# One matmul for both halves of the operand in the feed-forward input products of a float32 transformer stack

## The reference

```python
# first block
h2 = rms_norm(x, norm2_g)                                  # x * rsqrt(mean(x*x) + 1e-6) * norm2_g
x = x + jnp.square(jax.nn.relu(h2 @ w_ff1)) @ w_ff2        # 1024 -> 4096 -> 1024
# second block, in each of its two layers
x = layer_norm(ALPHA * x + swiglu(x, w_gate, w_up, w_down), g, b)
def swiglu(x, w_gate, w_up, w_down):                       # 1024 -> 2816 -> 1024
    return (jax.nn.silu(x @ w_gate) * (x @ w_up)) @ w_down
```

## Time and profile before

| | |
|---|---|
| time, median of 3 runs | 1293.88 us (1293.78 to 1297.35) |
| time of the profiled execution | 1296.51 us |
| its span, first to last instruction | 1294.7 us |
| PE busy | 1277.6 us (99%) |
| POOL busy | 947.9 us (73%) |
| ACT busy | 644.8 us (50%) |
| DVE busy | 411.5 us (32%) |
| PE's share of the chain that ended last | 96% |
| instructions on PE (matmul, and as many weight loads) | 8551 |
| HBM read | 216.07 MB |

### The profile page before, as it was taken

How to read it: one execution, slowest core, us unless ns; L and a number is a source line. 1 busy time by engine, 2 the same in 40 slices (tenths; PEclk the granted TensorE clock), 3 DMA queues, 4 the chain that set the end, 5 groups by cost and what they waited for, 6 DMA issues and landing times.

```text
span 1294.7 us, 20311 instructions
## 1 busy us (share of the span) xinstructions
PE 1277.6 (99%) x8551; PEld 1135.6 (88%) x8551; DVE 411.5 (32%) x747; ACT 644.8 (50%) x829; POOL 947.9 (73%) x417
## 2 busy tenths in 40 slices
PE   9999999999999999999999999999999989999997
PEld 7988878878889998899899789999879869999886
DVE  5535324542122210037653140101042662101025
ACT  5573535755455543344544454444345655444442
POOL 6856337846969889875578688787957657886983
PEclk9999989999999999999999999999999999999999
DMA  8735235634646656654456676656648435563651
GB/s 282 207 111 164 67 98 146 188 104 118 224 146 199 192 183 205 182 169 117 147 145 197 209 227 194 177 148 193 222 129 271 149 114 165 177 191 116 232 194 49
DMA packets 119056, 218.44 MB, mean 169 GB/s; under 512 B 9479, under 2 KB 22070, under 8 KB 118966
## 3 DMA queue, kind: packets, MB, share of 16 engines
q1 hardware_dynamic: 114976, 209.73, 52.7%
q10 hardware_dynamic: 3990, 7.42, 1.7%
HBM read 216.07 MB, written 1.05 MB: 168 GB/s over the span
## 4 chain that ended last, share of the span: by engine, by line
PE 96%; DVE 2%; DMA 1%; issue 0%; POOL 0%; ACT 0%; POOLq 0%; ACTq 0%; DVEq 0%
PE acc L1927 13%; PE acc L1929 13%; PE acc L1930 13%; PE acc L1920 13%; PE acc L1922 12%; PE acc L1921 12%; PE pm L1935 8%; PE acc L1876 2%; PE acc L1877 2%; PE acc L1878 2%; PE pm L1838 1%; PE acc L2116 1%; PE acc L2117 1%; PE acc L2118 1%; DMA ct<-in_consts 1%; PE pm L2412 1%
## 5 line engine op out<-in xcount | busy, mean ns | idle before, releaser
L559 POOL TENSOR_TENSOR wlo<-raw,whi 128x1024 fp32r<-128x1024 f32 (+4 forms) x412 | 947.1, 2328 | 333.8 <-ACT whi L574 332.3
L574 ACT ACTIVATE whi<-raw 128x1024 fp32r<-128x1024 f32 (+4 forms) x412 | 411.1, 1019 | 335.8 <-PE acc L1922 138.7
L1927 PE MATMUL acc<-XThi,whi 128*128 128x256 f32 x1400 | 398.2, 284 | 0.0
L1929 PE MATMUL acc<-XTlo,whi 128*128 128x256 f32 x1400 | 396.7, 283 | 0.0
L1930 PE MATMUL acc<-XThi,wlo 128*128 128x256 f32 x1400 | 396.7, 283 | 0.0
L1927 PEld LDWEIGHTS acc<-XThi,whi 128*128 128x128 f32 x1400 | 269.3, 192 | 1.1 <-issue 0.6
L1929 PEld LDWEIGHTS acc<-XTlo,whi 128*128 128x128 f32 x1400 | 269.4, 192 | 0.2
L1930 PEld LDWEIGHTS acc<-XThi,wlo 128*128 128x128 f32 x1400 | 269.2, 192 | 0.0
L1920 PE MATMUL acc<-whi,XThi 128*128 128x512 f32 (+4 forms) x320 | 123.7, 387 | 0.0
L1922 PE MATMUL acc<-whi,XTlo 128*128 128x512 f32 (+4 forms) x320 | 120.1, 375 | 0.0
L1921 PE MATMUL acc<-wlo,XThi 128*128 128x512 f32 (+4 forms) x320 | 120.0, 375 | 0.0
(11 more groups left out here) (404 smaller groups left out, 1705.8 us busy)
## 6 DMA issues: line engine op xcount, KB each, us to landing
raw<-in_w_in SPq DMA_DIRECT2D x68, 512.0 KB, 3.7
raw<-in_w_ff SPq DMA_DIRECT2D x64, 512.0 KB, 3.7
raw<-in_w_down SPq DMA_DIRECT2D x44, 512.0 KB, 3.8
raw<-in_w_gate SPq DMA_DIRECT2D x40, 512.0 KB, 3.7
raw<-in_w_up SPq DMA_DIRECT2D x40, 512.0 KB, 4.1
raw<-in_w_in_mix SPq DMA_DIRECT2D x36, 512.0 KB, 3.7
raw<-in_w_branch SPq DMA_DIRECT2D x16, 512.0 KB, 3.3
raw<-in_w_out_mix SPq DMA_DIRECT2D x16, 512.0 KB, 3.7
```

Of the source, the lines that this page charges most:

```text
L559: nc.gpsimd.tensor_tensor(wlo[:, u % SPLIT, 0:nk, 0:width], raw[:, u % RAW, 0:nk, 0:width], whi[:, u % SPLIT, 0:nk, 0:width].bitcast(F32), ...
L574: return nc.scalar.activation(out_, in_, func, **k)
L1927: T.matmul(o, wh[:, fs], hi[:, k, :], start=opens and f % 2 == 0, stop=False, skip_group_check=True)
L1929: T.matmul(o, wh[:, fs], lo[:, k, :], start=False, stop=False, skip_group_check=True)
```

## The change

It has three parts.

1. A new form B takes the place of F for f1, fg and fu. `XThi` and `XTlo` become the two parts of one tensor `XT`. For each k-tile and 128 features the high half of the weights is loaded once and meets both parts in one matmul of 512 columns (256 of `XThi`, 256 of `XTlo`), which fills a bank; the low half meets `XThi` in a matmul of 256 columns that adds to the bank's first half. So a chunk is 256 features wide (two banks), and there are 16 chunks of f1 and 11 each of fg and fu a layer. A unit of form B is four k-tiles by 256 columns, the same 512 KB in the same slot; a row of its transfer is 1 KB long, no more 2 KB.
2. The two halves of a bank are summed when it is read out: DVE copies the second half to SBUF and adds the first. In f1 the sum goes to `f1r`, and ACT takes Relu, Square (both to the PSUM bank `pm[:, 3]`) and the copy to `FFhi`. In the SwiGLU, ACT's Silu reads `sg` in SBUF, DVE writes up and then the product to `pm[:, 3]`.
3. The norm factor leaves f1: since relu(r x)^2 = r^2 relu(x)^2 for r > 0, DVE scales f2's rows with rstd^2 when it adds them to `X` (`scaled`). The matmuls `pm<-ct,rs` and ACT's copy to `rb` are gone, and DVE refines rstd behind f1's second chunk.

The first two chunks of f1 are interleaved by unit around the second half of `turn("x2")`.

```diff
-        for c in range(-(-DFF2 // W)):
-            w = min(W, DFF2 - c * W)
-            g.append((f"fg{i}_{c}", f"w_gate{i}", KD, c * W, w, "F"))
-            g.append((f"fu{i}_{c}", f"w_up{i}", KD, c * W, w, "F"))
+        for c in range(DFF2 // HW):
+            g.append((f"fg{i}_{c}", f"w_gate{i}", KD, c * HW, HW, "B"))
+            g.append((f"fu{i}_{c}", f"w_up{i}", KD, c * HW, HW, "B"))
...
+                        elif mode == "B":
+                            for f in range(width // P):
+                                fs = slice(f * P, (f + 1) * P)
+                                T.matmul(acc[:, n % 2, f, :], wh[:, fs], XT[:, :, k, :], start=opens, stop=False)
+                                last = T.matmul(acc[:, n % 2, f, 0:TOK], wl[:, fs], XThi[:, k, :], start=False,
+                                                stop=done)
...
-            for c in range(DFF // W):
+            for c in range(DFF // HW):
                 high_halves(landed(f"f1_{c}") + AHEAD)
-                act.wait_ge(S["f1_r"], c + 1)
+                act.wait_ge(*evac_at(f"f1_{c}"))
                 if c >= 1:
 
                     act.wait_ge(S["f1_lo"], c)
-                link(fn(f1s[:], f1r[:], ACT.Square))
-                fn(FFhi[:, 4 * c:4 * c + 4, :], f1s[:], ACT.Copy).then_inc(S["f1_hi"], 1)
+                link(fn(f1s, f1r[:], ACT.Relu))
+                link(fn(f1s, f1s, ACT.Square))
+                fn(FFhi[:, 2 * c:2 * c + 2, :], f1s, ACT.Copy).then_inc(S["f1_hi"], 1)
...
+                link(V.tensor_copy(f1r[:], accB(f"f1_{c}", 1)))
+                V.tensor_tensor(f1r[:], accB(f"f1_{c}", 0), f1r[:], ALU.add).then_inc(evac_at(f"f1_{c}")[0], 1)
                 v.wait_ge(S["f1_hi"], c + 1)
...
-            added("f2_0", 0)
+            def scaled(name, c):
+
+                v.wait_ge(S["w_used"], landed(name))
+                for t in range(NT):
+                    x = X[:, t, c * W:(c + 1) * W]
+                    last = V.scalar_tensor_tensor(out=x, in0=accT(name)[:, t], scalar=rs[:, 8 + t:9 + t], in1=x,
+                                                  op0=ALU.mult, op1=ALU.add)
+                last.then_inc(evac_at(name)[0], 1)
...
-            product("f1_0", XThi, XTlo, 1, ready=turned("x2"))
-            pe.wait_ge(S["xn"], 2)
-            for t in range(NT):
-                last = mm(pm[:, 0, t * P:(t + 1) * P], rs[:, t:t + 1].to_broadcast([P, P]), ident)
-            last.then_inc(S["r_row"], 1)
-            for c in range(1, DFF // W):
+            product("f1_1", XThi, XTlo, 0, 1, ready=turned("x2"), used=0)
+            product("f1_0", XThi, XTlo, 1, ready=turned("x2"), used=2)
+            product("f1_1", XThi, XTlo, 1, ready=turned("x2"))
+            for c in range(2, DFF // HW):
                 product(f"f1_{c}", XThi, XTlo)
```

More of the change, by code:

```diff
@@ L145, in gemm_plan @@
         first, k0 = len(units), k0[0] if k0 else 0
-        for k in range(0, kt, UK):
-            units.append((w, k0 + k, min(UK, kt - k), c0, width))
+        for k in range(0, kt, STEP[mode]):
+            units.append((w, k0 + k, min(STEP[mode], kt - k), c0, width))
         if name not in PARTIAL:
@@ L459, in build, with piece @@
             arrived.append(per_slot[u % RAW])
+        def piece(buf, u):
+            _, _, nk, _, width = units[u]
+            slot = buf[:, u % (RAW if buf is raw else SPLIT)]
+            if nk > UK:
+                slot = slot.rearrange("p u (h w) -> p (u h) w", w=width)
+            return slot[:, 0:nk, 0:width]
         def landed(name):
@@ L480, in accF, with accB @@
             return acc[:, n % 2].rearrange("p b (f t) -> p (b f) t", t=TOK)[:, 0:w // P, :]
+        def accB(name, part):
+            n, _, _, _, w, _, _ = chunks[name]
+            return acc[:, n % 2, 0:w // P, part * TOK:(part + 1) * TOK]
+        f1s = pm[:, 3, :].rearrange("p (f t) -> p f t", t=TOK)
+        hm = pm[:, 3, :].rearrange("p (f t) -> p f t", t=TOK)
         GATES = (0, 2, 1, 3)
@@ L590, in high_halves @@
                         act.wait_ge(S["w_used"], u - SPLIT + 1)
-                    fn(whi[:, u % SPLIT, 0:nk, 0:width], raw[:, u % RAW, 0:nk, 0:width],
-                       ACT.Copy).then_inc(S["w_hi"], 1)
+                    fn(piece(whi, u), piece(raw, u), ACT.Copy).then_inc(S["w_hi"], 1)
                     split[0] += 1
@@ L864, in _ @@
             for t in range(NT):
-                last = fn((f1s, f1r)[t][:].rearrange("p f t -> p (f t)"), X[:, t, :], ACT.Square, accum_out=ss[:, t:t + 1])
+                last = fn(f1q[:, t, :], X[:, t, :], ACT.Square, accum_out=ss[:, t:t + 1])
             link(last)
@@ L1906, in product @@
                 for u in range(first + start, end if stop is None else first + stop):
-                    if ready is not None:
-                        pe.wait_ge(*ready(u - first))
                     pe.wait_ge(S["w_lo"], u + 1)
-                    s = u % SPLIT
                     for i in range(units[u][2]):
-                        k = UK * (u - first) + i
-                        wh, wl = whi[:, s, i, 0:width], wlo[:, s, i, 0:width]
+                        k = STEP[mode] * (u - first) + i
+                        if ready is not None and i % UK == 0:
+                            pe.wait_ge(*ready(k // UK))
+                        wh, wl = piece(whi, u)[:, i, :], piece(wlo, u)[:, i, :]
                         done, opens = ends and k == kt - 1, begins and k == 0
```

99 lines of the change are left out of this document (50 added, 49 removed).

## The result

The changed kernel takes 1284.42 us, median of 4 runs (1284.05 to 1285.75), where the kernel before, in the same comparison, takes 1294.29 us (4 runs, 1293.78 to 1297.35). The ratio is 0.992, 95% interval 0.9908 to 0.9932: by the ratio 10.4 us less, with an interval of 8.8 to 11.9 us (the medians lie 9.9 us apart). I had forecast 1281.0 us, 12.9 us less, and a range of 1277 to 1288. The direction, the place and the mechanism came out; this first size is some 3 us short, and the experiments show that it isn't one size.

The account below looks back on a forecast made before the run. PE's gapless matmul stream was taken as the bound. Savings of 12.5 us (form B) and 0.4 us (norm factor) sum to 12.9 us, taking the median 1293.88 us to 1281.0 us, with an 8-in-10 range of 1277 to 1288 us.

Parts of the forecast that it names:

- The bound: Whole kernel: PE holds 96% of the chain, so a change counts only through PE's matmul stream or by starving it.
- The term of form B: f1 and SwiGLU input products on PE: 960 groups at 0.347 us instead of 0.360, saving 12.5 us.
- form T's price: 512-column matmuls with XThi stationary take 0.227 us, with FFhi 0.232; 0.227 was taken for form B's merged matmul.
- The norm factor's 0.44 us: Matmuls `pm<-ct,rs` on the chain: they go, saving 0.4 us.
- Read-out: DVE and ACT reading out chunks: f1's longest loop, 4.1 us, fits in 5.55; fg and fu also cost nothing.
- POOL: Unit pipeline: POOL needs 2.40 us a unit and holds PE's pace of 2.78; no cost.
- DMA: Weight transfers: 512 KB of 1 KB rows land in 5.6 us at most, refilled 13.9 us ahead; hidden.
- turns: PE reaches later k-tiles sooner in f1 and the SwiGLU; f1 has 0.4 us to spare; no cost.
- f2's rows: Two scaled additions of about 0.7 us replace one of 1.23 on DVE, ending before PE turns; no cost.
- Rival 1: Merged matmuls on PE: the fixed part is not saved; 1291.1 us, or 1293.4 with nothing saved; chance 0.10.
- Rival 2: Unit pipeline: POOL becomes the bound, kernel slower above 2.91 us a unit, 1308 us at 3.0; chance 0.06.
- Rival 3: The 60 smaller chunks: late read-outs or turns make PE wait, say 0.1 us each, giving 1287 us; chance 0.06.

Follow-up runs that it names:

- f1 alone: The change made in the first feed-forward only, with the norm factor on f2's rows and the SwiGLUs as in the kernel before: 1290.62 us, ratio 0.9973.

## Why the prediction was right, and where its size was not

- **The bound, and that only PE's stream counts: right.** PE has 97% of the chain, no idle time is put down ahead of L1947 or L1948, and undoing the merging alone gives all of it back (1293.92 against 1294.5 us).
- **The term of form B, 0.227 + 0.120 = 0.347 us a group, 12.5 us: right in size at the fast level, too large where a stream runs slow.** Measured 0.3467 in f1 and the first SwiGLU (8.1 us), and 0.3533 or 0.3467 in the second, depending on the execution (2.3 or 4.7 us): 10.4 or 12.8 us. The split inside the pair was not 0.227 and 0.120 but 0.230 and 0.117, or 0.232 and 0.115 as a mean; why the sum is the same is not shown, and that much was luck.
- **The step that failed is the carrying over of form T's price.** The choice of 0.227 over 0.232 was read rightly from the rows: in this kernel form T has 0.2267 with XT stationary and 0.232 or more with every other tensor, even within one stretch without a pause. But it is the price of a stream of one width. From it I gave form B one price, and form B with the same XT has two, 0.3467 and 0.3533 us a group. None of the rows that I took has a stream of mixed widths, so the open question was the mix, and I gave 0.232 (0.352 us a group, near the slow level's 0.3533) only a corner of the range.
- **The norm factor's 0.44 us:** too small to be told apart. f1 alone with it gained 3.5 us (2.1 to 4.8), the sum is 3.8.
- **Read-out, POOL, DMA, turns, f2's rows at nothing: right,** each by its rows above: a loop of 4.0 us (4.1 forecast) in 5.55, 2.38 us a unit, 3.8 to 4.0 us to landing, 0.4 us to spare at f1's turn as worked out.
- **Rival 1 (fixed part not saved) did not come.** A merged matmul saves 13.3 or 6.7 ns. Two measurements give 10.4 and 14.0 us in all, by the ratios. By the Trainium skill's rule (TensorE: Matmul & The Clock Gate, Back-to-back issue gap) the estimate is 2.8 us in all; the float32r rows here do not agree with it.
- **Rival 2 (POOL) did not come:** 2.38 us a unit, 0.5 us short of the 2.91 that it needed. **Rival 3 (small waits) did not come,** though 1284.4 us, short of the forecast, could be taken for a milder case of it. The distances tell the two apart: 0.3533 as the mean throughout the second SwiGLU, and no gap at a chunk's end.
- **Both medians, 1284.42 and 1281.0, lie in the range of 1277 to 1288,** and the second is the forecast, in part by luck: the forecast takes every stream at the fast level, and the kernel does not always run so. The profile at that median has all three stages fast.

## What to carry to other kernels

Where TensorE runs without a gap, merging two float32r matmuls that share their stationary operand saves a fixed part, here 13 ns of 120 or, at the slow level, 7, and it pays even when twice as many read-outs of half the size are added beside it, as long as those fit in the time of a chunk. When two rows of a trace give two prices for one kind of instruction, look first for a stretch without a pause in which the operand changes, as the one from BR to XT, and then measure the new mix of instructions in a stream of its own: a price read in one kind of stream need not hold in another. And before a difference of a few us is put down to a change, take a second profile of the same kernel: here it moved by 3.4 us.

## What the runs showed of the hardware

- A gapless stream of float32r matmuls of alternating width (512, 256) settles into one of repeating patterns, of 0.3467 us a pair (the columns plus 26.7 ns) or of 0.3533 (plus 33.3 ns), and stays there for up to 352 pairs. A foreign matmul throws it over in 14 of 20 cases in the kernel. Two profiles of the same program have the second SwiGLU at different levels. What decides it is open.
- 256 columns alone always took 0.120 us. 512 columns alone always took 0.2267 us in a stream of their own. In the kernel they took 0.2267 us with XT stationary and 0.2324 or 0.2333 with any other tensor, the change coming with the tensor within a stretch without a pause. For f2 and fd that is more than 5 ns on 912 matmuls, 5 us. What it is about these tensors is open: FF alone, at another place in SBUF, took 0.2267.
- Two high halves and then two low ones: 0.3483 us a pair alone and in the kernel, at every start.
